# First attention of a two-block fp32 kernel: when PSUM banks are given back, and where the softmax divisions stand

## The chip, the cores and the metric

One core of one Trainium2 chip runs the whole program. The metric is the device time of one execution in microseconds (us): the median of three runs was 1284.85 us (1284.74 to 1285.68). TensorE is called PE here, VectorE DVE, ScalarE ACT, GpSimd POOL and SyncE SP, as in the profile.

## The reference

Two transformer blocks run over one sequence of 512 tokens with 1024 features, all in float32. The change touches only the attention of the first block. That attention has two kinds of heads, 8 of each, in two groups that share keys and values:

```python
# sliding window (SWA): one softmax with a sink, window of 128
prob = e / (sum(e) + exp(sink - m));  o_swa = prob @ v
# native sparse (NSA): three softmaxes over the same query
o_c = (softmax(q k_cmp - slope dist) * valid) @ v_cmp       # 31 compressed keys
o_s = softmax(q k_slc - slope dist) @ v_slc                 # selected blocks: here all of them
o_w = softmax(q k_win - slope dist) @ v_win                 # window of 512
o   = g0 * o_c + g1 * o_s + g2 * o_w
mix = concat([o_nsa, o_swa]) @ w_o;  x = x + rmsnorm(mix, attn_post_g)
```

With 512 tokens every selected block and the whole window are in reach, so each of the two big NSA softmaxes is an ordinary causal one. Then follow the feed-forward of the first block, an embedding gate, and a second block (neighbourhood attention, retention, feed-forward). All of this is unchanged.

## The kernel before

Activations lie feature-major in SBUF, and each matrix product in full precision is made of three products of fp32r halves (`high*high`, `low*high`, `high*low`; lines 594 to 596). A weight matrix comes in pieces of 128x512: SP loads a piece, ACT rounds it to `wh` (L1324), and DVE (L2028) or POOL (L2949) makes the rest `wl`. PE then spends twelve matmuls of 512 columns on it.

The first attention is written by hand as a software pipeline over 28 **units**. Units 0 to 7 are SWA (pair j = u//2, group g = u%2). Units 8 to 27 are four rounds of five: `cmp`, `sl`, `wn`, `sl`, `wn` (compressed, both groups at once; selected and window of group 0; the same of group 1). So units 8, 13, 18 and 23 are compressed; the 24 others are called wide. One pass of the loop is a **step** s, and in it each engine does one stage of several units, in a fixed order that nothing rearranges at run time:

- **PE** (loop at L893): the dense pieces that `FILL1` gives to this step, transposes of unit s-2 (`turn1`, L814; compressed L855), scores of unit s+1 (`scores1`, L800/L801; compressed L844), values of unit s-3 (`values1`, L827/L828, and the compressed term L867). Steps 13, 14, 18, 19, 23, 24 and those after 27 have no dense piece.
- **DVE** (loop at L2307): `soft1(s)` reads the scores out of PSUM, adds the bias and takes the row extreme (L2197, four instructions; compressed L2239 to L2247); `out_add` (L2220) adds the two halves of the output of unit s-4; `out_low` (L2225); `rest1(s-3)` makes the low half of the transposed probabilities (L2213, from a PSUM bank); `norm1(s-1)` makes the reciprocals of a wide unit (L2278) or, for a compressed unit, the whole division (L2266 to L2272). After it come low halves of new queries and keys.
- **ACT** (loop at L1544): exponentials of unit s with their sums (L1510, compressed L1553), the high half of one weight piece (`hi`, L1324), high halves of the transposed probabilities of unit s-2 (`turned`, L1516), the copy of a finished product with `w_o_swa` out of its bank (`evicted`, L1531), the first half of an output (`out_part`, L1521).
- **POOL** (loop at L2977): multiplies the probabilities of unit s-1 by reciprocal and gate, four instructions (L2975), and makes the low half of the piece of the step before (L2949).

PE's transposes of unit u wait for POOL's four multiplications, those wait for DVE's reciprocals, and those for ACT's exponentials.

**Banks.** PSUM has 8 banks, and the kernel hands them out in a queue, fixed when the program is built:

```python
def take(self, key):
    b = self.free.pop(0)
    ...
def give(self, key):
    self.free.append(self.of[key])
```

`give` may stand before the bank's reader is done: `take` then returns a semaphore wait for the last reader, and PE waits for it before its first write. So the place of `give` in the loop decides which earlier user a bank had, and through it for whom PE waits. Scores of a wide NSA unit take three banks, its transposes three; an SWA unit takes two and two, a compressed one one and one; an output (`ob`) and a dense piece pair take one each.

Of the kernel before, what the change touches and what calls it, by code (L numbers as in the profile page):

```python
# [251 lines left out]
def build(nc, ins, out):  # L252
    ctx = ExitStack()
    with ctx:
# [278 lines left out]
        def closes(u):  # L533
            return unit(u)[0] in ("swa", "wn")
# [49 lines left out]
        def tensor(e):  # L584
# [275 lines left out]
            def values1(u):  # L860
                kind, j, g = unit(u)
                ob = out_key(u)
                if kind == "cmp" or kind == "sl" and g == 1:
                    c = unit_of("cmp", j, 0)
                    b, free = bank.take(ob)
                    e.wait_ge(*free, s_tl.at((c, 0)), s_ql.at("vc"))
                    m = t.matmul(b[:, :], VC[g][:, :], pct[:, :], start=True, stop=False, skip_group_check=True)  # L867
                if kind == "cmp":
                    m.then_inc(*s_pv.up(u))
                else:  # L870
                    n = ("sl", "wn", "swa").index(kind)
                    values(SWA if kind == "swa" else NSA, u, PT[buf_of(u)], lambda kb: high_and_low(V1[kb], n, g), ob,
                           kind == "swa", closes(u), s_xl.at(("v1", 3)))
                    if closes(u):
                        bank.give(ob)

# [11 lines left out]
            def swa_out(k):  # L888
                return [s_xl.at(("ob", "swa", k - 4))]

            scores1(0)
            later = []
            for s in range(N_UNITS + 3):  # L893
                if s < N_UNITS:
                    give_scores(s)
                if s >= 3:
                    give_turned(s - 3)
                for name, i in FILL1.get(s, ()):
                    key, n = fill_info(name, i)
# [5 lines left out]
                    if n == 1:  # L905
                        later.append(key)
                if s == 1:
# [3 lines left out]
                if s + 1 < N_UNITS:  # L911
                    if s + 1 == 8:
                        comp_values()
                    scores1(s + 1)
                for key in later:
                    bank.give(key)
                later.clear()
                if s >= 3:
                    values1(s - 3)

            def nsa_out(k):
# [389 lines left out]
        def scalar(e):  # L1311
# [232 lines left out]
            for s in range(N_UNITS + 4):  # L1544
# [18 lines left out]
                if s == 2:  # L1563
                    comp_keys()
                for name, i in later:
                    behind(name, i)
# [9 lines left out]
                if s == 7:  # L1576
# [5 lines left out]
                    m.then_inc(*s_qh.up("vc"))  # L1582
                for name, i in FILL1.get(s, ()):
                    if name == "w_o_swa":
                        evicted(i)
                if 3 <= s < N_UNITS + 3 and closes(s - 3):
# [428 lines left out]
        def vector(e):  # L2015
# [244 lines left out]
            def norm1(u):  # L2260
                kind, j, g = unit(u)
                s4 = S4[u % 6]
                if kind == "cmp":
# [8 lines left out]
                    v.tensor_tensor(p3, p3, s8.unsqueeze(3).broadcast_to([P, 2, 4, 31]), ALU.mult).then_inc(*s_nm.up(u))  # L2272
                else:
                    e.wait_ge(s_ex.at(u))
                    if kind == "swa":
                        v.tensor_tensor(s4, s4, G4[u % 6], ALU.add).then_inc(*s_nm.up(("s", u)))
                        e.wait_ge(s_nm.at(("s", u)))
                    v.reciprocal(s4, s4).then_inc(*s_nm.up(("r", u)))  # L2278

# [27 lines left out]
            for s in range(N_UNITS + 4):  # L2307
                for name, i in later:
                    behind(name, i)
                for name, i in later:  # L2310
                    filled(name, i)
                if s < N_UNITS:
                    soft1(s)
# [15 lines left out]
                if 3 <= s <= N_UNITS + 2:  # L2329
                    rest1(s - 3)  # L2330
                if 1 <= s <= N_UNITS:
                    norm1(s - 1)
                if s == 3:
# [931 lines left out]
```

## Time and profile before

| What | Value |
|---|---|
| median of 3 runs | 1284.85 us |
| profiled execution | 1282.31 us, span 1280.4 us |
| mean granted PE clock | 0.999 |
| PE busy | 98% of the span |
| DVE, ACT, POOL busy | 61%, 51%, 17% |

The span runs from the first to the last instruction; the profiled execution's own time is 1.9 us more. Matmuls overlap and their ends are modelled, so a PE that is shown busy can still start its next matmul late. The first attention takes the stretch from about 60 to 225 us; steps 8 to 30 are in 104 to 225 us.

### The profile page before, as it was taken

The page shows a single profiled execution, that of the slowest core. Times are in us where ns is not written, and L with a number is a line of the kernel's source. Part 1 is how long each engine was busy: PE and PEld are TensorE (multiplying, and loading weights), DVE is VectorE, ACT ScalarE, POOL GpSimd, SP SyncE. Part 2 cuts the span into 40 slices and gives each one's busy share as a digit, 9 for nine tenths or more (in the row PEclk, how much of TensorE's full clock was granted, in tenths as well). Part 3 has the DMA queues.
Part 4 walks back from the last instruction along what each step waited for, and adds up shares of the span by engine and source line. Part 5 has one row for each costly group of instructions (what it writes and reads, how often), then busy time and mean ns, then how long its engine had stood idle before and what let it go on. Part 6 is the DMA issues. An engine that isn't in the chain of part 4 may idle for free.

```text
span 1280.4 us, 16447 instructions
## 1 busy us (share of the span) xinstructions
PE 1260.2 (98%) x6004; PEld 1042.5 (81%) x6004; DVE 785.4 (61%) x1465; ACT 647.5 (51%) x1261; POOL 218.4 (17%) x234
## 2 busy tenths in 40 slices
PE   9999899999999999999999999999999999999998
PEld 8888788878888888888787777887888888888887
DVE  6689877676545565356878877588644343344334
ACT  6788777554344433233545645486633252332344
POOL 0075555001100010001002101032311030110111
PEclk9999999999999999999999999999999999999999
DMA  8211111423333333332423212432333323233332
GB/s 282 80 50 42 34 33 42 163 83 106 99 95 96 99 91 99 99 94 63 124 83 99 83 58 66 126 117 63 99 99 99 93 78 118 75 115 93 97 89 67
DMA packets 64625, 118.20 MB, mean 92 GB/s; under 512 B 7712, under 2 KB 12192, under 8 KB 64288
## 3 DMA queue, kind: packets, MB, share of 16 engines
q1 hardware_dynamic: 62704, 112.86, 29.0%
q10 hardware_dynamic: 1840, 4.29, 1.1%
q8 instruction: 48, 0.79, 0.3%
q14 instruction: 33, 0.27, 0.1%
HBM read 115.02 MB, written 2.10 MB: 91 GB/s over the span
## 4 chain that ended last, share of the span: by engine, by line
PE 88%; DVE 7%; issue 2%; ACT 2%; POOL 1%; DMA 0%; POOLq 0%; DVEq 0%; ACTq 0%
PE bank L594 25%; PE bank L596 25%; PE bank L595 25%; PE bank L814 2%; PE bank L694 2%; PE bank L696 2%; PE bank L695 2%; PE bank L800 1%; PE bank L827 1%; PE bank L801 1%; PE bank L828 1%; POOL pp L2975 1%; DVE q2p L2197 1%; DVE ptl L2213 1%; PE bank L768 1%
## 5 line engine op out<-in xcount | busy, mean ns | idle before, releaser
L2028 DVE TENSOR_TENSOR wl<-raw,wh 128x512 fp32r<-128x512 f32 (+2 forms) x360 | 267.4, 754 | 325.5 <-ACT wh L1324 324.8
L1324 ACT ACTIVATE wh<-raw 128x512 fp32r<-128x512 f32 (+1 forms) x398 | 242.3, 618 | 284.7 <-PE bank L596 274.0
L594 PE MATMUL bank<-AH,wh 128*128 128x512 f32 (+1 forms) x848 | 331.2, 391 | 2.1 <-DVE AL L2042 0.8
L596 PE MATMUL bank<-AH,wl 128*128 128x512 f32 (+1 forms) x848 | 329.5, 389 | 0.0
L595 PE MATMUL bank<-AL,wh 128*128 128x512 f32 (+1 forms) x848 | 327.7, 386 | 0.0
L594 PE MATMUL bank<-BH,wh 128*128 128x512 f32 x624 | 246.9, 396 | 1.2 <-ACT acc L1531 1.2
L596 PE MATMUL bank<-BH,wl 128*128 128x512 f32 x624 | 244.9, 393 | 0.0
L595 PE MATMUL bank<-BL,wh 128*128 128x512 f32 x624 | 243.7, 391 | 0.0
L594 PEld LDWEIGHTS bank<-AH,wh 128*128 128x128 f32 x848 | 159.5, 188 | 36.5 <-issue 2.9
L595 PEld LDWEIGHTS bank<-AL,wh 128*128 128x128 f32 x848 | 159.4, 188 | 33.5 <-issue 0.2
L596 PEld LDWEIGHTS bank<-AH,wl 128*128 128x128 f32 x848 | 159.3, 188 | 33.4
L594 PEld LDWEIGHTS bank<-BH,wh 128*128 128x128 f32 x624 | 117.3, 188 | 28.2 <-issue 1.9
L596 PEld LDWEIGHTS bank<-BH,wl 128*128 128x128 f32 x624 | 117.3, 188 | 26.1
L595 PEld LDWEIGHTS bank<-BL,wh 128*128 128x128 f32 x624 | 117.3, 188 | 25.9 <-issue 0.5
L2991 POOL TENSOR_TENSOR BL<-tmp,BH 128x512 fp32r<-128x512 f32 x22 | 28.6, 1298 | 354.4 <-ACT BH L1638 354.4
L3019 POOL TENSOR_TENSOR AL<-tmp,AH 128x512 fp32r<-128x512 f32 x32 | 40.6, 1304 | 269.6 <-ACT AH L1960 269.6
L2949 POOL TENSOR_TENSOR wl<-raw,wh 128x512 fp32r<-128x512 f32 x38 | 50.0, 1319 | 83.7 <-ACT wh L1324 83.6
L1510 ACT ACTIVATE pp<-pp,small 128x128 f32<-128x128 f32 (+2 forms) x96 | 50.2, 525 | 14.4 <-DVE small L2197 14.0
L2975 POOL TENSOR_SCALAR pp<-pp,small,gates 128x128 f32<-128x128 f32 (+1 forms) x64 | 40.8, 651 | 45.1 <-DVE small L2278 45.1
L2811 DVE TENSOR_TENSOR X<-X,bank 128x512 f32<-128x512 f32 x46 | 31.5, 686 | 24.3 <-PE bank L596 24.2
L2875 DVE SCALAR_TENSOR_TENSOR tmp<-bank,r_bc 128x512 f32<-128x512 f32 x32 | 22.0, 691 | 27.6 <-PE bank L596 16.1
L2975 POOL TENSOR_SCALAR pp<-pp,small,ones 128x256 f32<-128x256 f32 (+1 forms) x32 | 23.1, 734 | 78.4 <-DVE small L2278 78.4
(356 smaller groups left out, 1619.5 us busy)
## 6 DMA issues: line engine op xcount, KB each, us to landing
raw<-in_w_dn SPq DMA_DIRECT2D x104, 256.0 KB, 2.6
raw<-in_w_gu SPq DMA_DIRECT2D x88, 256.0 KB, 2.6
raw<-in_w_up SPq DMA_DIRECT2D x64, 256.0 KB, 2.6
raw<-in_w_nsa SPq DMA_DIRECT2D x16, 256.0 KB, 2.7
raw<-in_w_pg SPq DMA_DIRECT2D x16, 256.0 KB, 2.6
raw<-in_w_naq SPq DMA_DIRECT2D x16, 256.0 KB, 2.7
nbi<-in_na_bias ACTq DMA_DIRECT2D x8, 448.0 KB, 3.5
raw<-in_w_swa SPq DMA_DIRECT2D x10, 256.0 KB, 2.7
```

Source lines behind the costliest of these rows:

```text
L594: t.matmul(o, w, xh, start=start, stop=False, skip_group_check=skip)
L595: t.matmul(o, w, xl, start=False, stop=False, skip_group_check=skip)
L596: return t.matmul(o, wl, xh, start=False, stop=stop, skip_group_check=skip)
L694: t.matmul(o, x.h[:, c], w.h[:, 0:N], start=k == 0, stop=False)
L1324: a.activation(W[i % NW].h[:, 0:n], RAW[i % NRAW][:, 0:n], ACT.Copy).then_inc(*s_wh.up(i))
L1510: m = a.activation(o, o, ACT.Exp, bias=m4[:, qb:qb + 1], scale=-1.0, accum_out=s4[:, qb:qb + 1])
L2028: v.tensor_tensor(w.l[:, 0:n], RAW[i % NRAW][:, 0:n], w.h[:, 0:n], ALU.subtract).then_inc(*s_wl.up(i))
L2811: v.tensor_tensor(chunk(X, c), chunk(X, c), bank.ap(key)[:, :], ALU.add).then_inc(*s_sv.up(done))
L2949: g.tensor_tensor(w.l[:, 0:n], RAW[i % NRAW][:, 0:n], w.h[:, 0:n], ALU.subtract).then_inc(*s_wlg.up(i))
L2975: g.tensor_scalar(o, o, r, by, ALU.mult, ALU.mult).then_inc(*s_nmg.up((u, qb)))
L2991: g.tensor_tensor(x.l, tmp.ap(("u", k))[:, 0:T], x.h, ALU.subtract).then_inc(*s_xlg.up(("ff", k)))
L3019: g.tensor_tensor(x.l, tmp.ap(("rs", 8 * gi + k))[:, 0:T], x.h, ALU.subtract).then_inc(*s_xlg.up(("up", 8 * gi + k)))
```

## The change

Four things are altered, all inside the loop over the steps of the first attention.

1. Banks. The bank of a finished output was given back at once after its last values; now it is given a step later, after that step's transposed banks. The bank of a finished dense piece pair was given back at the end of its step; now it is given in the next step (ahead of the scores' banks where that step has no dense piece, otherwise after the transposed ones).
2. Reciprocals. For wide units from 9 on they move from the end of the DVE's step to its head, ahead of `soft1`. For units 0 to 7 they stay.
3. The compressed division moves from the end of the step after into the unit's own step, behind `rest1`.
4. ACT's copy `evicted` moves ahead of the piece's high half and of the transposed probabilities.

```diff
@@ PE @@
-                    if closes(u):
-                        bank.give(ob)
...
+            def give_all(keys):
+                for key in keys:
+                    bank.give(key)
+                keys.clear()
...
-            later = []
+            filled, summed = [], []
             for s in range(N_UNITS + 3):
+                if s not in FILL1:
+                    give_all(filled)
                 if s < N_UNITS:
                     give_scores(s)
                 if s >= 3:
                     give_turned(s - 3)
+                give_all(filled)
+                give_all(summed)
                 for name, i in FILL1.get(s, ()):
...
                     if n == 1:
-                        later.append(key)
+                        filled.append(key)
...
-                for key in later:
-                    bank.give(key)
-                later.clear()
                 if s >= 3:
                     values1(s - 3)
+                    if closes(s - 3):
+                        summed.append(out_key(s - 3))
+            give_all(summed)
@@ ACT @@
                 if s == 2:
                     comp_keys()
+                for name, i in FILL1.get(s, ()):
+                    if name == "w_o_swa":
+                        evicted(i)
                 for name, i in later:
                     behind(name, i)
...
-                for name, i in FILL1.get(s, ()):
-                    if name == "w_o_swa":
-                        evicted(i)
@@ DVE @@
+            def inverse1(u):
+                kind, j, g = unit(u)
+                s4 = S4[u % 6]
+                e.wait_ge(s_ex.at(u))
+                if kind == "swa":
+                    v.tensor_tensor(s4, s4, G4[u % 6], ALU.add).then_inc(*s_nm.up(("s", u)))
+                    e.wait_ge(s_nm.at(("s", u)))
+                v.reciprocal(s4, s4).then_inc(*s_nm.up(("r", u)))
...
+                if 9 < s <= N_UNITS and unit(s - 1)[0] != "cmp":
+                    inverse1(s - 1)
                 if s < N_UNITS:
                     soft1(s)
...
                     rest1(s - 3)
-                if 1 <= s <= N_UNITS:
-                    norm1(s - 1)
+                if 1 <= s <= 8:
+                    inverse1(s - 1)
+                if s < N_UNITS and unit(s)[0] == "cmp":
+                    norm1(s)
```

PE's instructions stand in the same order as before; their banks and waits differ. First place, PE in step 19: transposes of unit 17 (`ident,pp0`), scores of unit 20 (`ka_wn0`, `kb_wn0`), then the compressed term of unit 18. `s_ad` is raised by `out_add`, `s_sf` by `soft1`, `s_tl` by `rest1`, `s_nmg` by POOL's multiplications. Before:

```order
L814 MATMUL bank6<-ident_67,pp0_111 128x128 [waits s_nmg] x4
L814 MATMUL bank0<-ident_67,pp0_111 128x128 [waits s_ad]
L814 MATMUL bank0<-ident_67,pp0_111 128x128 x3
L814 MATMUL bank4<-ident_67,pp0_111 128x128 [waits s_sf]
...
L800 MATMUL bank3<-ka_wn0_94,ka_s0_86 128x512 [waits s_sf]
...
L800 MATMUL bank1<-ka_wn0_94,ka_s0_86 128x384 [waits s_sf]
...
L800 MATMUL bank2<-ka_wn0_94,ka_s0_86 128x256 [waits s_tl]
...
L867 MATMUL bank7<-pct_137,vc1_105 128x512 [waits s_tl]
```

And of the changed kernel:

```order
L814 MATMUL bank2<-ident_67,pp0_111 128x128 [waits s_nmg] x4
L814 MATMUL bank5<-ident_67,pp0_111 128x128 [waits s_sf]
L814 MATMUL bank5<-ident_67,pp0_111 128x128 x3
L814 MATMUL bank1<-ident_67,pp0_111 128x128 [waits s_sf]
...
L800 MATMUL bank4<-ka_wn0_94,ka_s0_86 128x512 [waits s_sf]
...
L800 MATMUL bank3<-ka_wn0_94,ka_s0_86 128x384 [waits s_tl]
...
L800 MATMUL bank0<-ka_wn0_94,ka_s0_86 128x256 [waits s_tl]
...
L867 MATMUL bank7<-pct_137,vc1_105 128x512 [waits s_tl]
```

The transposes no longer get an output's bank (`s_ad`); the second of the three score banks now comes from a transposed bank, as the third did before, and so waits for `rest1` of unit 16 (`s_tl`). Where the same wait stood before on the third bank, it was for an earlier part of that unit.

Second place, DVE from step 18 (compressed unit) into step 19. Before:

```order
L2247 TENSOR_TENSOR pc_113<-pc_113,small_66 128x2x4x31 [waits s_sf]
L2213 TENSOR_TENSOR ptl1_110<-bank3,pth1_109 128x512 [waits s_pv,s_th]
L2213 TENSOR_TENSOR ptl1_110<-bank1,pth1_109 128x512 [waits s_th]
L2213 TENSOR_TENSOR ptl1_110<-bank6,pth1_109 128x256 [waits s_th]
L2278 RECIPROCAL small_66<-small_66 128x4 [waits s_ex]
L2197 ISA pp1_112,small_66<-bank4,dn_70 128x512 [waits s_sc,s_tr]
```

And of the changed kernel:

```order
L2255 TENSOR_TENSOR pc_113<-pc_113,small_66 128x2x4x31 [waits s_sf]
L2221 TENSOR_TENSOR ptl1_110<-bank1,pth1_109 128x512 [waits s_pv,s_th]
L2221 TENSOR_TENSOR ptl1_110<-bank4,pth1_109 128x512 [waits s_th]
L2221 TENSOR_TENSOR ptl1_110<-bank2,pth1_109 128x256 [waits s_th]
L2273 TENSOR_REDUCE small_66<-pc_113 128x8 [waits s_ex]
L2275 RECIPROCAL small_66<-small_66 128x8 [waits s_nm]
L2277 TENSOR_TENSOR small_66<-small_66,gates_106 128x8 [waits s_nm]
L2279 TENSOR_TENSOR pc_113<-pc_113,small_66 128x2x4x31 [waits s_nm]
L2205 ISA pp1_112,small_66<-bank5,dn_70 128x512 [waits s_sc,s_tr]
```

The reciprocal of unit 17 has left (it stands ahead of the compressed scores' reading now), and the four instructions of the compressed division stand between `rest1` and the reading of the next unit's scores.

## Rows read from the trace of the kernel before

**Rows 1.** The page: busy time by engine

```profile
PE 1260.2 (98%) x6004; PEld 1042.5 (81%) x6004; DVE 785.4 (61%) x1465; ACT 647.5 (51%) x1261; POOL 218.4 (17%) x234
```

**Rows 2.** Busy time by stretch: from:to, length, then each engine's us, clock, DMA

```profile
100.00:120.00 20.00, 18.68 (x112) 15.88 (x111) 19.33 (x52) 15.99 (x43) 12.47 (x15) 1.00 0.12 41
120.00:140.00 20.00, 18.96 (x116) 16.16 (x115) 19.00 (x52) 17.32 (x47) 13.53 (x17) 1.00 0.17 43
160.00:180.00 20.00, 19.48 (x123) 17.16 (x122) 15.12 (x50) 14.02 (x42) 9.61 (x14) 1.00 0.14 40
```

**Rows 3.** PE's waits, 100 to 225 us: us in total, times, longest

```profile
PE bank L814 <- DVE os L2220: 2.7, 2, 1.4
PE bank L814 <- POOL pp L2975: 2.6, 7, 0.4
PE bank L594 <- ACT acc L1531: 1.2, 1, 1.2
```

**Rows 4.** PE in order of time: start, us, instruction, [idle before <- releaser]

```profile
116.10 0.55 PE L814 MATMUL bank<-ident,pp 128*128 128x128 f32 x3 [1.31 <-DVE os L2220]
...
142.65 1.31 PE L814 MATMUL bank<-ident,pp 128*128 128x128 f32 x10 [1.40 <-DVE os L2220]
...
159.05 0.50 PE L594 MATMUL bank<-BH,wh 128*128 128x512 f32 x1 [1.17 <-ACT acc L1531]
...
169.99 1.26 PE L814 MATMUL bank<-ident,pp 128*128 128x128 f32 x7 [0.42 <-POOL pp L2975]
...
172.36 0.39 PE L867 MATMUL bank<-pct,vc 128*128 128x512 f32 x1
...
220.61 0.98 PE L814 MATMUL bank<-ident,pp 128*128 128x128 f32 x7 [0.42 <-POOL pp L2975]
```

**Rows 5.** DVE in order of time, steps 18 to 20

```profile
164.01 0.48 DVE L2239 TENSOR_TENSOR pc<-bank,dc 128x124 f32<-128x124 f32 x2 [2.16 <-PE bank L844]
...
165.77 1.61 DVE L2213 TENSOR_TENSOR ptl<-bank,pth 128x512 fp32r<-128x512 f32 x3
...
167.38 0.65 DVE L2197 CUSTOM_DVE_ANT_0 pp<-bank,dn 128x512 f32<-128x512 f32 x1
...
169.63 0.68 DVE L2220 TENSOR_TENSOR os<-bank,os 64x512 f32<-64x512 f32 x1 [0.55 <-ACT os L1521]
170.24 1.60 DVE L2213 TENSOR_TENSOR ptl<-bank,pth 128x512 fp32r<-128x512 f32 x3
171.77 0.39 DVE L2266 TENSOR_REDUCE small<-pc 128x8 f32<-128x248 f32 x1
...
172.97 0.68 DVE L2197 CUSTOM_DVE_ANT_0 pp<-bank,dn 128x512 f32<-128x512 f32 x1
...
174.61 1.28 DVE L2213 TENSOR_TENSOR ptl<-bank,pth 128x512 fp32r<-128x512 f32 x2
```

**Rows 6.** DVE in order of time, steps 12 to 15

```profile
131.06 1.32 DVE L2225 TENSOR_TENSOR BL<-os,BH 128x512 fp32r<-128x512 f32 x1 [0.61 <-ACT BH L1525]
...
142.52 1.60 DVE L2213 TENSOR_TENSOR ptl<-bank,pth 128x512 fp32r<-128x512 f32 x3
...
145.25 0.68 DVE L2197 CUSTOM_DVE_ANT_0 pp<-bank,dn 128x512 f32<-128x512 f32 x1
```

**Rows 7.** ACT in order of time, first and last exponential of unit 14

```profile
141.78 0.71 ACT L1510 ACTIVATE pp<-pp,small 128x512 f32<-128x512 f32 x1
...
143.47 0.49 ACT L1510 ACTIVATE pp<-pp,small 128x256 f32<-128x256 f32 x1
```

**Rows 8.** ACT's copy of a product, 100 to 225 us: busy us, mean ns, idle

```profile
L1531 ACT ACTIVATE acc<-bank 128x512 f32<-128x512 f32 x8 | 4.7, 590 | 0.0
```

**Rows 9.** POOL in order of time

```profile
130.53 1.30 POOL L2949 TENSOR_TENSOR wl<-raw,wh 128x512 fp32r<-128x512 f32 x1
134.09 3.29 POOL L2975 TENSOR_SCALAR pp<-pp,small,gates 128x128 f32<-128x128 f32 x4 [2.27 <-DVE small L2278]
...
167.57 2.37 POOL L2975 TENSOR_SCALAR pp<-pp,small,gates 128x128 f32<-128x128 f32 x4 [1.99 <-DVE small L2278]
```

More of the change, by code:

```diff
@@ L914, in tensor @@
                     scores1(s + 1)
-                for key in later:
-                    bank.give(key)
-                later.clear()
                 if s >= 3:
                     values1(s - 3)
+                    if closes(s - 3):
+                        summed.append(out_key(s - 3))
+            give_all(summed)
+            later = []
             def nsa_out(k):
@@ L2261, in norm1 @@
                 kind, j, g = unit(u)
-                s4 = S4[u % 6]
                 if kind == "cmp":
@@ L2272, in norm1 @@
                     v.tensor_tensor(p3, p3, s8.unsqueeze(3).broadcast_to([P, 2, 4, 31]), ALU.mult).then_inc(*s_nm.up(u))
[L2273 to L2278, printed above, removed]
+            def inverse1(u):
[6 more added lines that the diff above has]
+                v.reciprocal(s4, s4).then_inc(*s_nm.up(("r", u)))
             def rest1(u):
```

## The prediction, made before the changed kernel ran

> **What bounds the kernel now.** I read the page first, then the busy time by stretch, then PE's waits in the first attention, and last the order of time of PE, DVE, ACT and POOL at those waits. PE is busy for 98% of the span [rows 1], and the granted clock is 1.00 in all stretches of the attention [rows 2], so the clock is no term. All that this change can win is PE's waiting between 100 and 225 us, all that it can lose is new waiting there: the dense work behind it hangs on the same PE stream and only shifts.
>
> The reader should see two things. First, PE's waits in that stretch are 2.7 us for banks whose last reader is DVE's addition of an output, 1.2 us for a bank that ACT copies out, and 2.6 us for POOL's multiplications [rows 3], 6.5 us in ten waits. The shown ends of matmuls are modelled and lie about a quarter of a microsecond after the next start that was possible, so ten waits stand for some 9 us of later starts. Second, DVE is busy 19.3 and 19.0 of 20 us in the two stretches from 100 to 140 us, more than PE itself (18.7 and 19.0), and only 15.1 of 20 in the stretch from 160 to 180 us [rows 2]. In steps 8 to 14 the pipeline has two full engines, and removing PE's wait for one DVE instruction leaves it waiting for the next.
>
> **The parts, and what each costs.** No instruction is added or removed. The sum is over places.
>
> *Banks of outputs and dense pieces.* The bank waits are those at 116.10 (1.31 us), 142.65 (1.40 us) and 159.05 (1.17 us) [rows 4]. With the new queue the transposes get banks that scores had, long read, and the second piece of `w_o_swa` gets one that was not just filled by the first: these three waits go. What is late next: scores of unit s+1 now mostly take the banks of the transposes of unit s-3, whose reader is `rest1(s-3)` in the same step of DVE. In step 19 that is the second score bank beside the third (the listing above), and the compressed term behind them waits for the last part of `rest1`.
>
> *Reciprocals at the head.* POOL's four multiplications take 2.37 us; for unit 17 they begin at 167.57 after 1.99 us of idleness, released by the reciprocal, and PE's transposes of unit 17 then wait for them at 169.99 [rows 9, 4]. At the head the reciprocal stands ahead of the reading of scores (1.6 us) and of `rest1` (1.6 us), so POOL starts 3 to 4 us earlier. All waits of PE for POOL go, but for part of the last (below). The added wait is DVE's, for the exponentials, and the whole step of DVE is queued behind it. In step 14 the last exponential ends at 143.96 (143.47 + 0.49) and the next reading of scores starts at 145.25 [rows 7, 6]: here, and in nearly all steps, DVE gets to the head later than ACT ends. I take 0 for it; upward the bound is the 2.2 us of a set of exponentials (141.78 to 143.96) in each of two or three steps without dense pieces, and I keep 1 us of it in the range.
>
> *The compressed division.* Its four instructions run from 171.77 to 172.97, 1.2 us, directly ahead of the reading of unit 20 [rows 5]. They now stand ahead of the reading of unit 19, at 167.38. The same work, but one step earlier on the engine that PE will be waiting for.
>
> *ACT's copy first.* The eight copies of 0.6 us [rows 8] now delay the high halves of transposed probabilities by as much. In steps with a dense piece PE spends twelve matmuls of 512 columns on it, at 2.4 GHz 12 x 0.21 = 2.6 us, which hides that; in the last step with a piece (27) it does not quite.
>
> Now the places, in order.
>
> - **Steps 8 to 14.** PE could start 1.6 us earlier at 116.10. But the division of unit 8 now comes before `rest1` of unit 6 and before the reading of unit 9, and DVE has no slack: `rest1(6)` ends about 1.2 us later, and the scores of unit 10 need its banks. In step 13, likewise, scores of unit 14 need banks of `rest1(10)`; in step 14 the scores of unit 15 need `rest1(11)` (at 142.52), which stands behind the reading of unit 14, now itself later by the division of unit 13 [rows 6]. Then the reading of unit 15 follows without a division, where before one stood. The waits for outputs and for POOL in this stretch (1.31, 1.40, and about 1.0 of the 2.6) come back as waits for `rest1`. Term: **0**, with -3.7 and +2.4 (two divisions that are not made good) as ends.
> - **Steps 15 to 20.** The wait at 159.05 goes: PE is 1.2 ahead. Compressed scores are read from 162.8 instead of 164.01. Then DVE needs, by the starts in its rows, 1.76 (reading, 164.01 to 165.77), 1.61 (`rest1`, to 167.38), 1.2 (division), 1.64 (reading of a wide unit, 172.97 to 174.61), 0.61 (`out_add`, 169.63 to 170.24), and 1.5 for `rest1` to be through with its last bank [rows 5]: 162.8 + 8.3 = 171.1, plus some 0.4 of ends and semaphores, is 171.5. PE's compressed term at 172.36 [rows 4] needs that bank. So it is about 0.8 us ahead, though 1.2 us for POOL also went before it. Term: **-0.8**, with -2.4 (both waits) as the far end.
> - **Steps 23 to 25.** The same pattern with the same lengths: what PE gains by POOL's waits is what DVE takes back. Term: **0**, far end -1.4.
> - **Steps 27 to 30.** Three short waits for POOL end at 220.61. POOL's last multiplications (2.4 us) come behind a weight piece's low half (1.3 us [rows 9]), which waits for its high half on ACT (about as long as the copy, 0.6 us), now behind such a copy [rows 8]. From the end of the exponentials that is 0.6 + 0.6 + 1.3 + 2.4 = 4.9 us, so this wait goes only in part, and then the last values wait for their `rest1`. Term: **-0.2**, far end -1.3.
>
> Sum: -1.0 us. Against the profiled execution that is 1282.31 - 1.0 = 1281.3 us; the median of the runs is 2.5 us above the profiled execution, so for the median 1284.85 - 1.0 = **1283.9 us**.
>
> *A rule against the trace.* DVE's `out_low` at 131.06 takes 1.32 us while POOL's subtraction runs at 130.53 for 1.30 us; POOL's four multiplications take 3.29 us at 134.09 but 2.37 at 167.57 [rows 6, 9]. My sum uses the undisturbed lengths for the moved instructions. The Trainium skill (SBUF — State Buffer, on the engine side of the ports) says that DVE and GpSimd share one pair of ports as an exclusive lock, taken by a DVE instruction with two SBUF inputs against a GpSimd one that reads SBUF, the loser blocked for the whole instruction. The rows fit that rule. By it the multiplications would do better beside the reading of scores (one input from PSUM) and the moved division might do worse.
>
> **The rivals.**
>
> *A, faster.* DVE is not as stiff as I think: POOL's slow multiplications and DVE's slow `out_low` beside them (0.9 us over 2.37, and of 1.32 about half [rows 6, 9]) vanish with the new positions, and DVE runs ahead by what it lost there. For it: DVE's busy time includes such blocked time. Against: in steps 8 to 14 only one or two such places exist. Half of the 9 us gives 1284.85 - 4.5 = 1280.4, all of it 1275.9.
>
> *B, slower.* The compressed division on the path. At each of four places (units 8, 13, 18, 23) the next reading of scores comes 1.2 us later, its exponentials too, and the reciprocal, now at the head, makes DVE wait for exactly those exponentials. If the step after does not give the 1.2 us back, that is +4.8, less 1.2 for the wait at 159.05: 1288.4. It decides once DVE reaches the reading of units 9, 14, 19 and 24 more than about 1 us later than PE would need. For it: rows 2 in the first stretch. Against: in the step after the division is missing, and DVE has 5 us per 20 to spare from 160 us on. [...]
>
> *C, nothing.* The bank queue only turns: waits move from one instruction to the other with no net difference, 1284.85 us.
>
> **The numbers.** About 0.2% (2.6 us) is what a measurement of this kernel can tell from no change. The forecast with its own ends (about -3 to +1.5) and C have 0.57, A 0.28, B 0.15. The range is 1280.0 to 1287.3: down to half of A's gain, up to a good half of B's loss. Faster by over 0.2% means half or more of A, or the lower end of the forecast: 0.29. Slower: B nearly whole, 0.14. Between: 0.57.
>
> **What would show it.** In the changed profile PE has no wait for `os` or for `acc` any more; POOL's multiplications of unit u begin within 0.5 us of the end of its exponentials or of POOL's own work; but scores, and the compressed terms behind them, wait for `ptl` of DVE in steps 8 to 14, 19 and 25, and DVE is still busy over 19 of 20 us up to 140 us. The last values of the attention start about 1 us earlier than before, and all of the rest is shifted by as much. I am wrong if those waits for `ptl` are small (A), if DVE idles for ACT at the head of steps, or if the division is shown much longer than 1.2 us (B).

## The result, and the profile of the changed kernel

| What | Before | Changed |
|---|---|---|
| median | 1284.85 us (1283.16 to 1287.28, 17 runs) | 1287.32 us (1285.03 to 1291.07, 17 runs) |
| profiled execution, its span | 1282.31, 1280.4 us | 1286.63, 1284.8 us |

The ratio of the runs is 1.0024, with a 95% interval of 1.0018 to 1.0030 (the two medians alone give 1.0019): slower by about 0.2%, 0.02 us above the predicted range (up to 1287.3) and on the other side of no change. PE, which does the same matmuls, is busy longer; the page of the changed kernel:

```profile
PE 1263.3 (98%) x6004; PEld 1043.5 (81%) x6004; DVE 789.5 (61%) x1465; ACT 648.7 (50%) x1261; POOL 219.5 (17%) x234
```

Both kernels have the same 6004 matmuls in the same order, so the n-th of one can be laid beside the n-th of the other. The table gives how much later a matmul starts than in before's trace, less what the execution was already late at 100 us. That part (1.3 us for the changed kernel, 0.8 to 2.6 us for others) comes mostly from the first 20 us, where the program is the same in all. I worked it out from the starts in the traces; a minus is a gain. The head row is the time in before's trace; steps 8 to 14 are up to 150, steps 15 to 20 up to 185, steps 23 to 25 up to 205.

```
kernel                      110    125    150    165    185    205    260
changed                   +0.96  +3.72  +2.81  +1.51  +2.80  +3.07  +2.98
banks alone               +0.93  +0.01  -0.28  -1.58  -1.66  -1.82  -1.75
reciprocals alone         +0.04  +0.03  -1.01  -1.01  -0.75  -0.88  -0.89
divisions alone           +0.04  +5.17  +4.12  +4.13  +4.89  +7.36  +7.74
copies first alone        +0.04  +0.04  +0.07  -1.33  -0.98  -0.95  -0.67
changed, divisions back   +0.93  +0.08  -1.30  -2.26  -2.62  -3.24  -3.46
changed, unit 8's back    +0.94  +0.11  -0.25  -1.55  -0.26   0.00  +0.27
changed, 13, 18, 23 back  +0.93  +2.47  +0.75  -0.57  -0.93  -1.56  -1.51
changed, behind the keys  +0.96  +1.15  +0.52  -0.78  +0.51  +0.76  +0.89
divisions back,
  rest1 first             -0.18  -1.59  -3.15  -4.44  -5.63  -7.08  -8.28
changed, second profile   +0.92  +3.68  +2.71  +1.41  +4.10  +4.35  +4.19
```

All of the loss is made by 125 us; then the kernel gains 2.2 us up to 165 and gives 1.3 back by 185. Behind the attention nothing changes in the changed kernel. PE's waits from 100 to 232 us, against [rows 3]:

```profile
PE bank L814 <- DVE small L2205: 3.5, 4, 1.8
PE bank L800 <- DVE ptl L2221: 3.0, 5, 0.9
PE bank L827 <- DVE ptl L2221: 0.4, 1, 0.4
```

The waits for `os`, `acc` and POOL are gone, all three. In their place PE waits for `ptl`, as forecast, and 3.5 us for what was not: transposes (L814) wait for DVE's reading of scores (L2205). The sum, 6.9 us, is about before's 6.5. PE in order of time, the places of [rows 4] and the new ones:

```profile
111.54 0.44 PE L800 MATMUL bank<-ka_sl,qs 128*128 128x384 f32 x1 [0.88 <-DVE ptl L2221]
...
118.52 0.55 PE L814 MATMUL bank<-ident,pp 128*128 128x128 f32 x3 [1.78 <-DVE small L2205]
...
145.49 1.56 PE L814 MATMUL bank<-ident,pp 128*128 128x128 f32 x10 [0.54 <-DVE small L2205]
147.72 0.50 PE L800 MATMUL bank<-ka_wn,qs 128*128 128x512 f32 x1 [0.66 <-DVE ptl L2221]
...
161.88 0.50 PE L594 MATMUL bank<-BH,wh 128*128 128x512 f32 x1
...
173.25 1.13 PE L814 MATMUL bank<-ident,pp 128*128 128x128 f32 x6 [1.01 <-DVE small L2205]
...
175.48 0.44 PE L800 MATMUL bank<-ka_wn,ka_s 128*128 128x384 f32 x1 [0.46 <-DVE ptl L2221]
```

161.88 is the matmul of 159.05 in before, now without its 1.17 us. DVE, for its part, now waits for exponentials at the head of its steps, which it never does between 100 and 232 us in before's trace:

```profile
DVE small L2288 <- ACT pp L1518: 5.7, 11, 0.9
```

Busy time by stretch, against [rows 2] (from:to, length, then PE, PEld, DVE, ACT, POOL, the clock, DMA share, GB/s):

```profile
100.00:120.00 20.00, 17.20 (x103) 14.32 (x102) 19.34 (x48) 13.19 (x35) 12.19 (x15) 1.00 0.13 41
120.00:140.00 20.00, 19.47 (x111) 17.12 (x110) 17.70 (x50) 19.26 (x53) 13.34 (x16) 0.91 0.14 41
160.00:180.00 20.00, 18.50 (x114) 15.87 (x113) 17.02 (x51) 16.14 (x47) 11.77 (x15) 1.00 0.14 40
```

PE is busy 1.5 us less than before up to 120 us, DVE as much as before; from 120 to 140 us the clock is 0.91, where it was 1.00; from 160 to 180 DVE is busy 1.9 us more, with hardly more to do.

What DVE and POOL do at the first of these waits (step 8 and the start of step 9). DVE:

```profile
112.15 0.38 DVE L2273 TENSOR_REDUCE small<-pc 128x8 f32<-128x248 f32 x1
...
113.01 0.58 DVE L2279 TENSOR_TENSOR pc<-pc,small 128x248 f32<-128x248 f32 x1
113.52 0.68 DVE L2118 TENSOR_TENSOR kb_wn<-tmp,ka_wn 64x512 fp32r<-64x512 f32 x1
114.21 0.87 DVE L2119 TENSOR_TENSOR kb_wn<-tmp,ka_wn 64x512 fp32r<-64x512 f32 x1
115.11 0.94 DVE L2118 TENSOR_TENSOR kb_wn<-tmp,ka_wn 64x512 fp32r<-64x512 f32 x1
116.07 1.67 DVE L2119 TENSOR_TENSOR kb_wn<-tmp,ka_wn 64x512 fp32r<-64x512 f32 x1
117.76 0.69 DVE L2205 CUSTOM_DVE_ANT_0 pp<-bank,dn 128x512 f32<-128x512 f32 x1
```

POOL in the same stretch:

```profile
112.34 3.17 POOL L2989 TENSOR_SCALAR pp<-pp,small,ones 128x128 f32<-128x128 f32 x4 [3.86 <-DVE small L2288]
115.48 1.70 POOL L2963 TENSOR_TENSOR wl<-raw,wh 128x512 fp32r<-128x512 f32 x1
```

The division (112.15 to 113.59) lets POOL get going with unit 7's multiplications before DVE comes to the four low halves of the keys. These then take 4.2 us, from 113.52 to 117.74, where they took 2.8; PE's transposes wait behind them, at 118.52. ACT has nothing to do for 5.40 us until 119.53, and POOL nothing for 5.24 us until 122.42, so both feel it.

Behind that wait the clock falls. The changed kernel by single microseconds:

```profile
117.00:118.00 1.00, 0.00 (x0) 0.00 (x0) 0.97 (x2) 0.00 (x0) 0.18 (x1) 1.00 0.00 0
118.00:119.00 1.00, 0.48 (x3) 0.31 (x3) 1.00 (x5) 0.00 (x0) 0.00 (x0) 1.00 0.64 178
119.00:120.00 1.00, 0.86 (x5) 0.70 (x5) 0.97 (x5) 0.47 (x1) 0.00 (x0) 1.00 0.22 84
120.00:121.00 1.00, 0.47 (x5) 0.33 (x3) 0.97 (x3) 1.00 (x5) 0.00 (x0) 0.85 0.00 0
121.00:122.00 1.00, 1.00 (x4) 1.00 (x5) 1.00 (x3) 1.00 (x5) 0.00 (x0) 0.50 0.00 0
```

It stays at 0.50, which is 1.2 GHz, until 124 us, with PE at full work from 121 us on.

A second place shows how long a division can be. DVE in step 18, then POOL:

```profile
170.80 1.34 DVE L2277 TENSOR_TENSOR small<-small,gates 128x8 f32<-128x8 f32 x1
172.17 0.42 DVE L2279 TENSOR_TENSOR pc<-pc,small 128x248 f32<-128x248 f32 x1
172.50 0.68 DVE L2205 CUSTOM_DVE_ANT_0 pp<-bank,dn 128x512 f32<-128x512 f32 x1
```

```profile
170.82 1.28 POOL L2963 TENSOR_TENSOR wl<-raw,wh 128x512 fp32r<-128x512 f32 x1
```

A product of 128 x 8 numbers, 0.17 us elsewhere, takes 1.34 us: it ends at 172.14, and POOL's subtraction beside it at 172.10. From the first start of its four instructions to the last end the division takes 1.44 us for unit 8, 2.04 for 13, 2.46 for 18 and 1.57 for 23; in before's trace it takes 1.29 to 1.30 at all four. In every trace the reduction and the reciprocal, which read one tile, keep 0.37 to 0.41 and 0.20 us, also beside POOL; what is stretched is one of the two products, which read two tiles in SBUF. For unit 18 it is L2277, above; for unit 13 in number 8 below it is L2279, 1.46 us from 142.30 instead of 0.42, beside a subtraction of POOL that ends at 143.48.

### The profile page after: what moved, and what is told of

It is laid out like the page before. It is cut to its first block, busy times and chain, and to the rows that moved or that the text cites. A ratio compares the mean times of both kernels' runs of the same rounds, so it can differ in the third digit from the quotient of the medians.

```text
span 1284.8 us, 16451 instructions
## 1 busy us (share of the span) xinstructions
PE 1263.3 (98%) x6004; PEld 1043.5 (81%) x6004; DVE 789.5 (61%) x1465; ACT 648.7 (50%) x1261; POOL 219.5 (17%) x234
## 4 chain that ended last, share of the span: by engine, by line
PE 89%; DVE 7%; issue 2%; ACT 1%; DMA 1%; SPq 0%; POOL 0%; POOLq 0%; ACTq 0%; DVEq 0%
PE bank L594 25%; PE bank L596 25%; PE bank L595 25%; PE bank L694 2%; PE bank L695 2%; PE bank L696 2%; PE bank L814 2%; PE bank L800 1%; PE bank L827 1%; PE bank L828 1%; PE bank L801 1%; DVE ptl L2221 1%; DVE q2p L2205 1%; PE bank L768 1%; DMA raw<-in_w_ple 1%
```

## The experiments

From the traces I held **theory D**: the moved compressed divisions are the loss, since DVE reads the next scores later by them. Its rivals were **B**, the new order of the banks (new waits for `ptl` and `L2205`), and **H**, DVE waiting for exponentials at the head of its steps. Numbers 1 to 4 take the parts one by one. "Before" is the kernel before, run on the same chip as the experiment: 1284.1 us in the first eight runs, 1284.25 in the last four, where beside the changed kernel it was 1284.85. Medians of different groups are therefore compared by their distance to their own "before".

**1. The banks alone.** Part 1 of the change, on the kernel before; nothing else.

```diff
-                    if closes(u):
-                        bank.give(ob)
...
+                if s not in FILL1:
+                    give_all(filled)
...
+                give_all(filled)
+                give_all(summed)
```

> Theory D (the compressed division, now ahead of the next reading of scores, is the loss): the new bank queue alone loses nothing; DVE's waits for outputs at steps 9 and 14 turn into waits for the reading of scores or for rest1, the one for ACT's copy goes: 0 to -3 us against the kernel before. Theory B (the bank queue is the loss: transposes now take a bank whose scores are read in the same step, scores take a bank that rest1 frees in the same step): +1 to +3 us, with PE waits of 3 us or more for the reading of scores and for ptl.

Measured: 1282.76 us, ratio 0.9992 (0.9983 to 1.0001). The table has it lose 0.9 us at 110 us, where scores wait for `ptl`, and win 2.7 later. PE's waits for `os` and for `acc` are gone, those for POOL stay (2.7 us). So the bank queue is no loser.

**2. The reciprocals alone.** Part 2, on the kernel before.

```diff
+                if 9 < s <= N_UNITS and unit(s - 1)[0] != "cmp":
+                    inverse1(s - 1)
                 if s < N_UNITS:
                     soft1(s)
```

> Reciprocals at the head alone, divisions, banks and ACT's order as before. Theories D and B agree: PE's 2.6 us of waits for POOL go, DVE waits little at the head: -1 to -3 us. If DVE's wait for the exponentials at the head is the loss (theory H), +1 to +3 us, with DVE idle for ACT's pp in no-piece steps.

Measured: 1283.74 us, 0.9994 (0.9985 to 1.0003); 0.9 us gained in the trace. DVE does wait at the head for the exponentials, 4.4 us in five waits of up to 0.9, so H has its mechanism, but not its loss: between 100 and 232 us DVE now waits 3.9 us for PE's scores, where it was 8.3 in before. PE's waits for POOL are gone, and those for `os` grow from 2.7 to 4.6 us.

**3. The divisions alone.** Part 3, on the kernel before.

```diff
-                if 1 <= s <= N_UNITS:
-                    norm1(s - 1)
+                if 1 <= s <= N_UNITS and unit(s - 1)[0] != "cmp":
+                    inverse1(s - 1)
+                if s < N_UNITS and unit(s)[0] == "cmp":
+                    norm1(s)
```

> Compressed divisions in their own step alone. Theory D: +2 to +5 us; the reading of unit 9 begins 2 to 3 us later than before, POOL's multiplications of unit 7 and DVE's low halves of keys beside them take longer. Theory B: within 1 us of the kernel before.

Measured: 1291.22 us, 1.0054 (1.0042 to 1.0067), slower than the changed kernel itself. Its waits of PE, 100 to 232 us:

```profile
PE bank L814 <- DVE os L2220: 7.0, 4, 4.1
PE bank L814 <- POOL pp L2980: 2.3, 7, 0.4
PE bank L594 <- ACT acc L1531: 1.2, 1, 1.2
```

With the banks as before, the transposes of unit 7 stand behind an addition that DVE reaches still later: 4.1 us in one wait, and the clock at 0.50 from 119 to nearly 126 us. Another fall follows at 204 to 208.

**4. The changed kernel with its divisions back.**

```diff
-                if s < N_UNITS and unit(s)[0] == "cmp":
-                    norm1(s)
+                if 1 <= s <= N_UNITS and unit(s - 1)[0] == "cmp":
+                    norm1(s - 1)
```

> The changed kernel with the divisions put back to the end of the next step. Theory D: 3 to 6 us faster than the changed kernel, so -1 to -3 us against the kernel before. Theory B: still at least 1 us slower than the kernel before.

Measured: 1281.01 us, 0.9975 (0.9966 to 0.9984). The other parts together are a gain of 0.25%, and the moved divisions cost 5.6 us: the changed kernel stands 2.5 us above its own "before", this one 3.1 below (the two medians as they are differ by 1287.32 - 1281.01 = 6.3, the two traces by 6.4). The waits left, of PE, 100 to 232 us:

```profile
PE bank L800 <- DVE ptl L2221: 3.0, 5, 0.9
PE bank L827 <- DVE ptl L2221: 0.4, 1, 0.4
```

DVE at the place of the changed kernel's wait of 1.78 us: the low halves at their own length, the reading right behind.

```profile
113.21 0.65 DVE L2118 TENSOR_TENSOR kb_wn<-tmp,ka_wn 64x512 fp32r<-64x512 f32 x1
...
115.30 0.69 DVE L2119 TENSOR_TENSOR kb_wn<-tmp,ka_wn 64x512 fp32r<-64x512 f32 x1
116.02 0.69 DVE L2205 CUSTOM_DVE_ANT_0 pp<-bank,dn 128x512 f32<-128x512 f32 x1
```

Less the 2.42 us that this execution was late, the reading starts at 113.60; in the changed kernel (1.33 us late) at 116.43. That is 2.83 us, for a division of 1.44.

**5. The copies first, alone.** Part 4, on the kernel before: the two lines of `evicted` ahead of `behind`.

> The kernel before with one thing done: ScalarE copies the two banks of w_o_swa's pieces ahead of the evictions and exponentials of the same step. The banks alone gave about -1.4 us and the reciprocals alone -0.4 us, while the changed kernel with its divisions back stands at -3.1 us, so about -1.3 us has no part to its name yet. If the copies first are worth it, this kernel stands at 1282.8 us and TensorE's wait of 1.2 us for a copy of acc (L1531) before 200 us is gone. If they are worth nothing alone, it stands at 1284.1, and the parts of the change help one another (a wait taken away by one part is only of use when the others are away too).

Measured: 1283.71 us, 0.9991 (0.9982 to 1.0000), and the wait for `acc` is gone. By its median it lies nearer to "worth nothing alone" than to 1282.8. The gains of the three parts alone are 1.75, 0.89 and 0.67 us in the traces, together 3.3, where the three in one kernel have 3.46 (by the medians 2.1 against 3.1, within the noise). But they do not simply add: the banks alone and the copies alone take away the same wait for `acc`, 1.3 us in either row of the table at 165, which one kernel can gain only once. Up to 165 us the kernel with all three is 1.7 us short of the sum; behind it, it gains another 1.2 us, where the three alone lose 0.6 together.

**6. Unit 8's division back, the others in their own steps; 7. the reverse.**

```diff
+                if s == 9:
+                    norm1(8)
-                if s < N_UNITS and unit(s)[0] == "cmp":
+                if 8 < s < N_UNITS and unit(s)[0] == "cmp":
                     norm1(s)
```

> The changed kernel, with unit 8's division alone at the end of step 9, those of units 13, 18 and 23 still in their own steps. Theory D8 (the loss lies in step 8 and what follows from it: the key's low halves, TensorE idle, its clock at 0.50): no stretch of the attention below 1.00 in the clock but for small ones, and 1281 to 1281.5 us, nearly all of the 5 us between the changed kernel and the one with all divisions back. Theory D4 (each of the four divisions costs alike, 1.2 to 1.6 us of VectorE ahead of the next scores): 1285.5 to 1286 us, a quarter of it regained.

Measured: 1286.03 us (1282.93 to 1288.45), 1.0013 (1.0003 to 1.0023).

> The mirror of the last: the changed kernel with the divisions of units 13, 18 and 23 back at the end of the next step, and unit 8's alone in its own step. D8: 1286 to 1287 us, with the wait of TensorE for VectorE's reading of unit 9's scores and the clock at 0.50 near 121 to 124 us as in the changed kernel. D4: 1282 to 1282.5 us.

Measured: 1284.54 us, 1.0001 (0.9992 to 1.0010). Neither theory holds as put: both halves cost. Against the kernel with all divisions back, unit 8's alone costs 3.5 us by the medians and 1.95 in the traces; the three others together cost 5.0 by the medians (3.6 when measured again, number 12) and 3.7 in the traces, by the table 1.05 at 150, 1.3 more at 185, 0.9 at 205, 0.5 at 260. Of the traces' difference between the changed kernel and number 4, 6.4 us, these two make 5.7. The sixth kernel's profile shows the clock at 1.00 all through the attention. In the seventh's, the wait for L2205 is again 1.8 us, and yet:

```profile
118.00:119.00 1.00, 0.00 (x0) 0.00 (x0) 0.97 (x2) 0.00 (x0) 0.28 (x1) 1.00 0.00 0
119.00:120.00 1.00, 0.39 (x3) 0.31 (x3) 1.00 (x5) 0.00 (x0) 0.00 (x0) 1.00 0.60 160
120.00:121.00 1.00, 0.86 (x5) 0.62 (x4) 0.97 (x7) 0.38 (x1) 0.00 (x0) 1.00 0.27 102
121.00:122.00 1.00, 0.55 (x5) 0.41 (x3) 0.97 (x3) 1.00 (x5) 0.00 (x0) 1.00 0.00 0
122.00:123.00 1.00, 0.91 (x5) 0.74 (x6) 1.00 (x3) 1.00 (x6) 0.00 (x0) 1.00 0.00 0
```

No fall. Up to step 12 this is the changed kernel's program, and at 125 us the two traces differ by 3.72 - 2.47 = 1.25 us: that is the fall's price. (This profiled execution is also the fastest of number 7's eleven.)

**8. Each division at the very end of its step,** behind the low halves of the keys.

```diff
                 for name, i in later:
                     filled_low(name, i)
+                if s < N_UNITS and unit(s)[0] == "cmp":
+                    norm1(s)
```

> The changed kernel with each compressed division at the very end of its own step, behind the four low halves of the keys in step 8. This tells the division's own 1.4 us from what it does to the low halves beside GpSimd (4.2 us for the four instead of 2.8, since GpSimd's multiplications of unit 7, released by the reciprocal, get ahead of them). Theory P (the meeting with GpSimd is needed for the loss): low halves at 0.65 to 0.70 us each, GpSimd's multiplications held to about 3.9 us, reading of unit 9's scores only 1.4 us later than with the divisions back, TensorE's wait there under 1 us and no fall of its clock: 1282 to 1283.5 us. Theory Q (any 1.4 us ahead of unit 9's reading is enough, the meeting is an ornament): the clock falls to 0.50 in step 9 again, 1286 us or more.

Measured: 1286.24 us, 1.0012 (1.0003 to 1.0020). The time is Q's, the trace of step 8 is P's. DVE there:

```profile
115.47 0.69 DVE L2119 TENSOR_TENSOR kb_wn<-tmp,ka_wn 64x512 fp32r<-64x512 f32 x1
116.18 0.41 DVE L2273 TENSOR_REDUCE small<-pc 128x8 f32<-128x248 f32 x1
...
117.08 0.69 DVE L2279 TENSOR_TENSOR pc<-pc,small 128x248 f32<-128x248 f32 x1
117.68 0.68 DVE L2205 CUSTOM_DVE_ANT_0 pp<-bank,dn 128x512 f32<-128x512 f32 x1
```

The low halves keep their 0.69 us, POOL's multiplications take 3.92, the reading comes 1.5 us later than in number 4, PE waits 0.4 us for it, not 1.8, and the clock stays up. At 125 us it is 1.07 us behind number 4, where kernel 7 is 2.39 behind: so the nearly bare division (its last product still takes 0.69 us beside POOL) is worth 1.1 us there, the meeting of the low halves with POOL another 1.3. What I had not reckoned is that the later three divisions, untouched by this edit, cost 3.3 of the 4.35 us between this kernel and number 4. P's mechanism is shown, its total was wrong.

**9. A version to beat both.** Number 4, and DVE reads the transposes' banks ahead of the outputs' addition and low half.

```diff
+                if 3 <= s <= N_UNITS + 2:
+                    rest1(s - 3)
                 if s >= 4 and closes(s - 4):
...
-                if 3 <= s <= N_UNITS + 2:
-                    rest1(s - 3)
```

> A version meant to be better than both kernels: the changed kernel with its divisions back (1281.0 us), and in each step VectorE reads the transposes' banks (L2221, the low halves of the turned probabilities) ahead of the addition and low half of the finished outputs, not behind them. All that TensorE still waits for in the attention are those readings: 3.0 us in five waits of its second banks of scores, and 0.4 us. The addition ahead of them takes 0.68 us, in the pair's steps another 0.67 us. If the additions are not due themselves, the five waits of up to 0.9 us shrink by about 0.7 us each and it stands at 1278 to 1279.5 us. If the outputs' banks are wanted at the step's end, the waits change their name (os L2228) and it stays at 1281 or becomes slower.

Measured: 1275.70 us (1274.52 to 1276.42, 5 runs), 0.9935 (0.9922 to 0.9947): faster than before by 0.65%, and more than I expected. What is left of PE's waits from 100 to 232 us:

```profile
PE bank L594 <- DVE small L2205: 1.1, 1, 1.1
PE bank L800 <- DVE ptl L2221: 0.3, 1, 0.3
```

Against number 4 the table gains 1.1 us by 110, 0.6 more by 125, 0.8 each by 185 and 205, and 1.0 by 260. Of the 4.8 us between the two traces the matched starts put 3.95 at five of number 4's six waits (shown with 3.05, so about 0.2 us of later start more for each, as in before). One new wait of 1.1 us, in a dense piece, takes 1.2 back between 125 and 150. The other 2 us lie in many smaller steps, each under 0.35 us, most of which the list of waits does not show: the largest is 0.32 us at the compressed scores of unit 18, of which number 4's trace shows 0.07 as a wait. So the list of waits understates what a late reader costs.

**10. Reciprocals at the head in all steps,** on number 4.

> The changed kernel with its divisions back, and the reciprocals of the first nine wide units at the head of the step too, not only the later ones. For it: GpSimd's multiplications begin about a step's length sooner there, and in step 8 they would be over before the low halves of the keys. Against it: TensorE never waited for GpSimd in steps 1 to 8, and VectorE, the busy engine there (19.3 of 20 us from 100 to 120 us), would stand at each head for ScalarE's exponentials (with a sliding unit's addition before the reciprocal). Those who hold that VectorE has no time to give expect 1281 to 1283 us; those who hold that early reciprocals are free gain, 1280 us or less.

Measured: 1281.99 us, 0.9985 (0.9976 to 0.9994), by the medians a microsecond worse than number 4, though the intervals of the two touch. Its matmuls lose 1.8 us between 80 and 100 us and win back part of it later. In the early steps DVE has no time to give.

**11 and 12. The changed kernel, and number 6, profiled again.**

> The changed kernel again, for a second profile. In its first the clock was granted 0.50 for 3 us after TensorE's wait for unit 9's scores; the kernel with unit 8's division alone in its own step had the same wait, and no fall. If the fall hangs on the program alone, it is here again, with the same 1.25 us behind it; if it comes in some executions and not in others, this profile may be without it, at a span about 1.2 us shorter (apart from the start), and the wide spread of this kernel's times (1285.0 to 1291.1 us) has its reason.

Measured: 1286.68 us, 1.0020 (1.0007 to 1.0033). The fall of step 9 is here again, from 120 to 124 us, and there is a second one that the first profile did not have, behind the wait of step 19:

```profile
172.00:174.00 2.00, 1.32 (x7) 0.92 (x8) 2.00 (x9) 0.34 (x1) 0.00 (x0) 1.00 0.43 131
174.00:176.00 2.00, 1.54 (x7) 1.13 (x5) 1.76 (x5) 1.98 (x9) 0.00 (x0) 0.71 0.00 0
176.00:178.00 2.00, 2.00 (x7) 1.71 (x8) 2.00 (x10) 1.47 (x4) 1.73 (x4) 0.50 0.03 8
```

In the table the two profiles of this program differ by 1.3 us at 185.

> The kernel with unit 8's division alone back, again, for a second profile. Its first was among its fastest executions (1284.1 us where the median was 1286.0 and the highest 1288.5), with the clock at 1.00 all through the attention. If falls of the clock are what spreads its times, a slower execution's profile shows stretches at 0.50, behind the waits of the steps of units 14, 19 and 24; if this execution is fast again, the spread stays open.

Measured: 1284.75 us, 1.0009 (0.9999 to 1.0019). This profiled execution took 1285.76 us and shows the fall at the same place, which its first (1284.14) had not:

```profile
170.00:172.00 2.00, 1.51 (x7) 0.82 (x7) 2.00 (x7) 1.54 (x5) 0.00 (x0) 0.99 0.13 50
172.00:174.00 2.00, 2.00 (x9) 1.81 (x8) 1.76 (x6) 1.98 (x7) 0.93 (x2) 0.50 0.00 0
```

So one program, with the same waits, has the fall in some executions and not in others. How often that happens can be read without a profile, since the mean granted clock of every execution is known. Profiles without a fall have 0.999, those with one 0.998 or 0.997, number 12's with two 0.996, number 11's with three 0.995 (a fall at the very end of the span, which all have, aside). All executions of three kernels:

| Kernel | Mean granted clock: mean time (executions) |
|---|---|
| changed | 0.999: 1286.4 us (5); 0.997: 1287.1 (7); 0.995: 1289.9 (5) |
| changed, unit 8's back (number 6) | 0.999: 1284.0 (2); 0.998: 1285.3 (5); 0.996: 1287.8 (4) |
| changed, divisions back (number 4) | 0.999 or 1.000: 1280.8 (11) |

So falls go with much of the spread, above all with the slowest executions: 12 of the changed kernel's 17 executions have a lower clock than 0.999, and none of number 4's. And they are not the whole loss: without one the changed kernel still takes 1286.4 us, above before's 1284.85. Where in the program the falls of the executions without a profile lie is not shown.

## Why the prediction was wrong

The sum of the terms was -1.0 us; the same places have +2.98 in the first trace. Two steps failed. The prediction held that the transposes get banks long read, and so overlooked PE's waits for the reading of scores; and it priced the moved division at its undisturbed 1.2 us, with nothing held up behind it, and so had steps 8 to 14 come out at 0. With the divisions back the same program gains 3.5 us in the trace instead of losing 3.0.

- **"Removing PE's wait for one DVE instruction leaves it waiting for the next."** Right, and the waits for `os` and `acc` went as said. The five for `ptl`, 3.0 us, came as said.
- **"The transposes get banks that scores had, long read."** This failed. In steps 9, 14, 19 and 24, behind each compressed unit, they get a bank whose scores are read in the very same step of DVE: 118.52, 145.49 and 173.25 above. That tied the transposes to the instruction that the moved division stands in front of. PE waited 3.5 us in all for it. With the divisions back, that wait is gone altogether (number 4), so the bank order alone does no harm.
- **"I take 0" for DVE's wait at the head.** The cost held, the reason did not. It was that DVE gets to the head later than ACT ends; in the changed kernel it waits there 11 times, 5.7 us in all, once (0.24 us, until 148.84) at the very place of the example, the head behind step 14. Number 2 has such waits too, and is not slower than before. **POOL's waits** went, the last one too, against my doubt in steps 27 to 30.
- **"1.2 us" for the division, and "undisturbed lengths for the moved instructions".** This is the term that was mis-sized. It takes 1.44 to 2.46 us beside POOL (from first start to the next instruction's start, as the prediction counted, 1.37 for unit 8 and 2.38 for unit 18), and in step 8 it holds up four further instructions by 1.4 us. I had the two rows of DVE and POOL slowing each other [rows 6, 9] and the Trainium skill's rule on them (SBUF — State Buffer), and used the undisturbed lengths all the same. A moved instruction changes not only its own neighbour but who starts first: in before, the low halves go first and POOL's multiplications take 3.92 us; with the division ahead, POOL goes first with 3.17, and DVE waits. The Trainium skill (SBUF — State Buffer, Who interferes with whom) says that the order of issue decides which of the two is blocked, and number 8 against number 7 agrees, with 1.3 us.
- **Steps 8 to 14: 0, at most +2.4.** Measured +2.8. Number 4 stands at -1.3 there; the bare division of unit 8 adds 1.1, its meeting with POOL 1.3, the clock 1.25 and unit 13's division 1.05. That makes 3.4, so 0.6 us less was measured than these add up to.
- **Steps 15 to 20: -0.8.** Measured 0.0. The 1.2 for `acc` came (-1.3 at 165), and 1.3 went again at 173 and 175, behind a division of 2.46.
- **Steps 23 to 25 and 27 to 30: 0 and -0.2.** Measured +0.3 and -0.1.
- **"The clock is no term."** Wrong as a method: before's clock of 1.00 said only that no fall came with its waits of up to 1.4 us. Behind a wait of 1.8 us it fell in two of three traces. That the wait is the cause is likely and not shown, since falls also come without one (below).
- **Rival B** had the mechanism and the place. Its time (1288.4) is near by luck in part: it had 4.8 us of loss and 1.2 of gain, where the traces have 6.4 and 3.5. It was given 0.15, for the reason that "in the step after the division is missing". It is, but that comes after PE has waited; and DVE's spare time lies elsewhere (in the changed kernel's trace it idles 1.49 us ahead of 153.70, and not once between 168.60 and 174.75). The head's waits for exponentials, in its reasoning, are not needed for a loss: number 3 has none of the early reciprocals and loses the most.
- **"12 x 0.21 = 2.6 us"** for a dense piece is 2.5, and eight such matmuls of before's trace stand 0.23 us apart (160.08 to 161.91), so it is 2.7. Nothing hangs on it.

Left open: how the later three divisions' 3.7 us divide between their own length and the meetings with POOL. Number 3, without reciprocals at the head, has divisions of 1.44 us at all four places, so early reciprocals and early divisions together make the long ones; no kernel took POOL's work away there.

## What to carry to other kernels

When instructions move on an engine that is full, ask for every bank or buffer handed on by the new order in which step its last reader stands, and look at what was put in front of that reader. Take moved VectorE work at its undisturbed length only where GpSimd is idle before and after the move. Once PE waits for a reader's place in an engine's order and not for its amount of work, changing the order inside the step can be worth more than the moves between steps: 5 us in number 9, for one statement moved ahead of two others. And take the mean clock of every execution into the comparison, not only that of the profiled one.

## What the hardware showed that I had not expected

- GpSimd can hold up a tiny VectorE instruction by its own whole length: 0.17 us became 1.34, ending 0.04 us after GpSimd's. By the shown starts VectorE was 0.02 us ahead there, so which of the two issued first cannot be read from them. Of the division's four instructions only the two with two inputs in SBUF were stretched so.
- The clock of TensorE fell to 1.2 GHz for 3 us behind a wait of 1.8 us, in two of three traces with that wait, and behind waits of at most 1.0 us in one of two profiles of number 6's program. Each of these falls cost 1.25 to 1.4 us. The Trainium skill (TensorE: Matmul & The Clock Gate, Part 1) describes the two rates, which the granted clock of 0.50 and 1.00 agrees with, and says that at a kernel's start the point of change varies between runs. Here more varies than the point: one of number 6's two profiles has the fall and the other has not.
- Falls also come where PE waits for nothing that the profile shows: in the second profile of the changed kernel near 765 us (1.6 us lost by the matched starts), while before's trace has none there. Those of numbers 2, 10 and 12 have one at the same matmuls, and numbers 6 and 8 one near 870 us (0.6 to 0.7 us lost); of one program (the changed kernel's, and number 6's) one profile has the fall and the other has not, so it belongs to the execution and not to an edit.
